# Two transformer blocks on one core: the dense up-projections by Strassen's seven products

## The reference, cut to what matters

```python
D_FF = 2816
def swiglu(h, w1, w3, w2):                                  # layer 0 of the first block
    return (jax.nn.silu(h @ w1) * (h @ w3)) @ w2

def channel_mixer(h, w_up, ffn_dw_w, ffn_dw_b, w_down):     # both layers of the second block
    u = causal_depthwise_conv(h @ w_up, ffn_dw_w, ffn_dw_b) # three taps over the tokens
    a, b = jnp.split(u, 2, axis=-1)
    return (jax.nn.silu(a) * b) @ w_down
```

## Time and profile before

| | |
|---|---|
| median of three runs | 2740.4 us (2736.98 to 2740.84) |
| profiled execution, its own time | 2740.35 us |
| its span, first to last instruction | 2738.2 us |
| granted TensorE clock, mean | 0.994 of full |
| busy share: TensorE, VectorE, ScalarE, GpSimd | 99%, 35%, 19%, 3% |
| the 20 F units of f13 | 296 to 434 us of the span |
| those of up0 | 1983 to 2122 us |
| those of up1 | 2520 to 2659 us |

### The profile page before, as it was taken

The page is one execution under the profiler, slowest core; times in us unless marked ns, Lnnn a source line. Parts: engine busy times, 40 slices in busy tenths (PEclk is TensorE's granted clock), DMA queues, the critical chain, the costliest instruction groups (busy, mean ns, idle before and its releaser), DMA issues. The chain is left out here.

```text
span 2738.2 us, 45257 instructions
## 1 busy us (share of the span) xinstructions
PE 2697.9 (99%) x19261; PEld 2103.6 (77%) x19261; DVE 968.6 (35%) x2203; ACT 528.6 (19%) x1128; POOL 94.2 (3%) x181
## 2 busy tenths in 40 slices
PE   7999999999989999999999999999999999999999
PEld 6788988978978745555546548788988997889888
DVE  2555432366520000001001004676555235744330
ACT  3322100232220001101101103333121024231110
POOL 0000111000100000000000000000011000000000
PEclk9999999999989999999999999999999999999999
DMA  9536675654569998999999995344576643234432
GB/s 371 195 139 246 230 265 215 233 210 162 185 276 427 404 367 352 426 427 409 426 426 408 426 394 226 130 146 174 211 276 237 231 171 139 93 127 158 169 116 100
DMA packets 70328, 706.62 MB, mean 258 GB/s; under 512 B 7793, under 2 KB 8049, under 8 KB 31601
## 3 DMA queue, kind: packets, MB, share of 16 engines
q1 hardware_dynamic: 44640, 610.92, 55.8%
q0 software_dynamic: 25488, 92.81, 9.5%
HBM read 702.65 MB, written 1.05 MB: 257 GB/s over the span
## 5 line engine op out<-in xcount | busy, mean ns | idle before, releaser
L990 PE MATMUL psum<-hT,ring 128*128 128x256 f32 x4544 | 994.4, 380 | 0.0
L990 PEld LDWEIGHTS psum<-hT,ring 128*128 128x128 f32 x4544 | 859.9, 190 | 121.5 <-ACT work L1596 2.0
L990 PE MATMUL psum<-work,ring 128*128 128x256 f32 x1624 | 353.0, 379 | 0.0
L990 PEld LDWEIGHTS psum<-work,ring 128*128 128x128 f32 x1624 | 308.2, 190 | 42.7 <-ACT work L1596 0.7
L2295 DVE CUSTOM_DVE_ANT_0 mod_in<-mod_in,c_rows,cols 128x1024 f32<-128x1024 f32 x152 | 190.8, 1279 | 40.0 <-DMA mod_in<-in_mods 36.7
L1251 PE MATMUL psum<-ring,work 128*32 128x256 f32 x2880 | 186.5, 380 | 0.0
L2256 DVE TENSOR_TENSOR work<-work,psum 128x128 f32<-128x128 f32 x119 | 34.3, 288 | 414.0 <-ACT work L1637 414.0
L2422 POOL DMA_DIRECT2D mod_in<-in_mods x176 | 93.5, 531 | 2464.7 <-DVE ada L2295 2419.2
L1005 PE MATMUL psum<-hT,ring 128*128 128x128 f32 x1408 | 164.7, 279 | 3.0 <-DVE hT L1908 1.9
L1005 PEld LDWEIGHTS psum<-hT,ring 128*128 128x128 f32 x1408 | 162.9, 195 | 3.6 <-DVE hT L1908 2.0
L1261 PE MATMUL psum<-ring,work 128*64 128x256 f32 x1280 | 147.0, 382 | 0.0
(11 more groups left out here) (262 smaller groups left out, 2472.6 us busy)
## 6 DMA issues: line engine op xcount, KB each, us to landing
ring<-in_m SPq DMA_DIRECT2D x112, 2048.0 KB, 16.5
work<-in_m SPq DMA_DIRECT2D x56, 2048.0 KB, 17.6
ring<-in_w_in SPq DMA_DIRECT2D x46, 2048.0 KB, 8.5
mod_in<-in_mods POOLq DMA_DIRECT2D x176, 512.0 KB, 5.4
ring<-in_up SPq DMA_DIRECT2D x22, 2048.0 KB, 8.1
ring<-in_f SPq DMA_DIRECT2D x11, 2048.0 KB, 9.0
ring<-in_down SPq DMA_DIRECT2D x16, 1408.0 KB, 6.7
ring<-in_w_o SPq DMA_DIRECT2D x8, 2048.0 KB, 8.5
```

What stands on the lines that cost most here:

```text
L990: last = mm(gbank(it["bank"])[:, j, :], wt[:, k, col0 + j * P:col0 + (j + 1) * P], rhs[:, k0 + k, :], start=(n == 0), stop=(n == total - 1))
```

## The change

Each of the 60 F units becomes a unit of mode S. Its weights (1024 x 256) and its tokens (1024 x 256) are cut into two by two blocks, and the product of the blocks is formed by seven products of half size instead of eight, in Winograd's form of Strassen's scheme. Each product is four matmuls of 128x128 weights with 128 tokens moving.

- GpSimd makes the sums of weights, four instructions of 128x512 for each unit, one unit ahead of TensorE: three into `MIXED` (room for two units) and one in place in the ring slot.
- VectorE makes the sums of tokens once for each stage, the new item `t_mix`: four instructions of 128x512.
- An S unit takes two of six PSUM banks (`FF_BANKS`). ScalarE copies the first product (128x128), and VectorE adds up the rest with four instructions: 128x256, 128x256, 128x256, 128x128. The silu, the taps and the product of halves come after that. The taps (`fir_rest`) read SBUF instead of PSUM and are put off by one unit.
- Ada items are moved: up0 has 16 instead of 34 and its `down` the next 8; up1 has none instead of 6. The mixer of layer 1 of the second block gets 24.

```diff
+    def s_unit(S, c, col, evac, load, free, first=False, last=False):
+        u = unit([(c, DK, 512, col, 0)], "h", evac, load, free, mode="S")
+        u.update(bank=(ff_bank(), ff_bank()), S=S, mix=state["mixed"], first=first, last=last)
...
-            out.append(unit([(c, DK, 512, 0, 0)], "h", ea, [c], []))
-            out.append(unit([(c, DK, 512, 256, 0)], "h", eb, [], [c]))
+            out.append(s_unit(S, c, 0, ea, [c], [], first=(i == 1)))
+            out.append(s_unit(S, c, 256, eb, [], [c], last=(i == nu - 1)))
...
+            items.insert(2, ph("t_mix", S="a0f", at="a"))
             plan.extend(spread(items, adas(0, 40, 48) + adas(1, 0, 28)))
...
-        if l == 0:
-            rest = adas(2, EARLY_MODS, 48)
+        rest = adas(2 + l, EARLY_MODS, 48)
...
-        plan.extend(spread(items, adas(3, 0, 34) if l == 0 else adas(3, 42, 48)))
+        items.insert(2, ph("t_mix", S=f"b{l}f", at="b"))
+        plan.extend(spread(items, adas(3, 0, 16) if l == 0 else []))
...
+    mixed = [it for it in plan if it["kind"] == "unit" and it["mode"] == "S"]
+    for n, it in enumerate(mixed):
+        it["before"] = mixed[n - 2]["g"] if n >= 2 else None
...
@@ TensorE @@
+            def mixed_unit(it):
...
+                product(one, 0, a[0][0], b11)
+                product(one, 1, a[0][1], b21)
+                if it["first"]:
+                    need(("t_mix", it["S"]))
+                need(("mixed", g, 2))
+                product(one, 2, sum2, t2).then_inc(tensor_done, w.step(("unit_one", g)))
+                if two in ev:
+                    need(ev[two])
+                ev[two] = ("evac", g)
+                product(two, 0, sum1, t1)
+                need(("mixed", g, 3))
+                product(two, 1, a[1][0], t3)
+                need(("mixed", g, 4))
+                product(two, 2, sum4, b22)
+                product(two, 3, a[1][1], t4).then_inc(tensor_done, w.step(("unit", g), *[("used", c["n"]) for c in it["free"]]))
...
@@ ScalarE @@
+            def mixed_unit(it):
...
+                need(("unit_one", g))
+                A(firsts[it["mix"] % 2], hbank(it["bank"][0])[:, 0, :], ACT.Copy).then_inc(scalar_done, w.step(("first", g)))
+                need(("evac", g))
...
@@ VectorE @@
+            def t_mix(it):
...
+                need(("h", S, 0, 3), ("h", S, 1, 3), ("h", S, 1, 7))
+                V.tensor_tensor(t1, b12, b11, ALU.subtract).then_inc(vector_done, w.step())
+                V.tensor_tensor(t3, b22, b12, ALU.subtract).then_inc(vector_done, w.step())
+                dve.wait_ge(vector_done, w.now() - 1)
+                V.tensor_tensor(t2, b22, t1, ALU.subtract).then_inc(vector_done, w.step())
+                dve.wait_ge(vector_done, w.now())
+                V.tensor_tensor(t4, b21, t2, ALU.subtract).then_inc(vector_done, w.step(("t_mix", S)))
...
+            def mixed_unit(it):
...
+                need(("first", g))
+                V.tensor_tensor(out[:, 0:2, :], firsts[it["mix"] % 2].unsqueeze(1).to_broadcast([P, 2, P]),
+                                hbank(one)[:, 1:3, :], ALU.add).then_inc(vector_done, w.step(("evac_one", g)))
+                need(("unit", g))
+                dve.wait_ge(vector_done, w.now())
+                V.tensor_tensor(sums, out[:, 1:2, :].to_broadcast([P, 2, P]), hbank(two)[:, 0:2, :], ALU.add).then_inc(
+                    vector_done, w.step())
+                dve.wait_ge(vector_done, w.now())
+                V.tensor_tensor(out[:, 1:3, :], sums, hbank(two)[:, 2:4, :], ALU.add).then_inc(vector_done, w.step())
+                V.tensor_tensor(out[:, 3, :], sums[:, 1, :], hbank(two)[:, 0, :], ALU.add).then_inc(
+                    vector_done, w.step(("evac", g)))
...
@@ GpSimd @@
+            def mix(it):
...
+                if it["first"]:
+                    pool.wait_ge(vector_done, w.at("x_mul", it["S"], 1, 4))
+                pool.wait_ge(slot_loaded[c["slot"]], w.at("loaded", c["n"]))
+                if it["before"] is not None:
+                    pool.wait_ge(tensor_done, w.at("unit", it["before"]))
+                add(sum1, a21, a22, ALU.add).then_inc(weights_mixed, w.step(("mixed", g, 1)))
+                pool.wait_ge(weights_mixed, w.now())
+                add(sum2, sum1, a11, ALU.subtract).then_inc(weights_mixed, w.step(("mixed", g, 2)))
+                add(a21, a11, a21, ALU.subtract).then_inc(weights_mixed, w.step(("mixed", g, 3)))
+                pool.wait_ge(weights_mixed, w.now() - 1)
+                add(sum4, a12, sum2, ALU.subtract).then_inc(weights_mixed, w.step(("mixed", g, 4)))
...
+                    if it["kind"] == "unit":
+                        while len(made) < len(ahead) and ahead[len(made)]["g"] <= it["g"] + 1:
+                            mix(ahead[len(made)])
+                            made.append(it["g"])
```

More of the change, by code:

```diff
@@ L130 @@
           "rope_tables", "tables", "consts", "mod_cols", "acol", "x_sq", "x_sum", "x_fin", "x_mul", "x_aff", "x_add",
-          "n_add", "c_add")
+          "n_add", "c_add", "t_mix")
+FF_BANKS = (0, 1, 2, 5, 6, 7)
+MIXES = 6
 def make_plan():
-    plan, state = [], {"chunk": 0, "bank": 0, "side": 0, "ada": 0, "fence": 0}
+    plan, state = [], {"chunk": 0, "bank": 0, "side": 0, "ada": 0, "fence": 0, "ff": 0, "mixed": 0}
     def chunk(name, idx, width):
@@ L261, in h_units, with glu_units @@
                      tile=u, ready=ready) for u in range(2)]
-    def glu_units(name, pre, nu, evacs, halves):
+    def glu_units(S, name, pre, nu, evacs, halves):
         out = h_units(chunk(name, pre + (0,), SLOT), DK, "h", halves)
+        for u in out:
+            u["bank"] = ff_bank()
+        out[1]["half_bank"] = out[0]["bank"]
         for i in range(1, nu):
@@ L432, in make_plan @@
             plan.extend(score(z + dq + dk + q + dv + v + hg + gates + pa + pb + o, slots))
-            items = glu_units("f13", (), FF_U, lambda i: (evac("glu_a", i), evac("glu_b", i)),
+            items = glu_units("a0f", "f13", (), FF_U, lambda i: (evac("glu_a", i), evac("glu_b", i)),
                               [evac("glu_h")] * 2)
@@ L548, in make_plan @@
         assert not taps
[L549 to L552 removed]
+        rest = adas(2 + l, EARLY_MODS, 48)
+        for j, it in zip((2, 3, 4, 5) + tuple(22 + 22 * j // (len(rest) - 4) for j in range(len(rest) - 4)), rest):
+            slots[j].append(it)
         slots[28] += [ph("c_add", tag=B, layer=l)]
@@ L970, in unit @@
                 g = it["g"]
[L972 to L975, removed]
+                if it["mode"] == "S":
+                    mixed_unit(it)
+                    return
+                if it["bank"] in ev:
+                    need(ev[it["bank"]])
+                ev[it["bank"]] = ("evac", g)
                 need(*it["ready"])
@@ L1018, in unit, with product @@
                 last.then_inc(tensor_done, w.step(("unit", g), *[("used", c["n"]) for c in it["free"]]))
+            def mixed_unit(it):
+                g, (one, two) = it["g"], it["bank"]
+                c = it["parts"][0][0]
+                a, (sum1, sum2, sum4) = quads(it)
+                b11, b12, b21, b22 = (R["h"][:, 4 * i:4 * i + 4, t * P:(t + 1) * P] for i in range(2) for t in range(2))
+                t1, t2, t3, t4 = TOKENS[it["S"][0]]
+                def product(bank, at, weights, tokens):
+                    for k in range(4):
+                        last = mm(hbank(bank)[:, at, :], weights[:, k, :], tokens[:, k, :], start=(k == 0), stop=(k == 3))
+                    return last
+                if one in ev:
+                    need(ev[one])
+                ev[one] = ("evac_one", g)
+                pe.wait_ge(slot_loaded[c["slot"]], w.at("loaded", c["n"]))
+                product(one, 0, a[0][0], b11)
[13 more added lines that the diff above has]
+                product(two, 3, a[1][1], t4).then_inc(tensor_done, w.step(("unit", g), *[("used", c["n"]) for c in it["free"]]))
             def first_mod(it):
@@ L2345, in run @@
                         acol_of(it)
+                    elif kind == "t_mix":
+                        t_mix(it)
                     elif kind == "x_add":
```

107 lines of the change are left out of this document (102 added, 5 removed).

## The result

The changed kernel takes 2786.0 us (median of four runs, 2783.6 to 2788.2) against 2739.4 us for the kernel before on the same chip: a ratio of 1.0172, with a 95% interval of 1.0159 to 1.0184. It is 1.7% slower. The forecast was 2785 us.

The account below looks back on a forecast made before the run. TensorE was taken to bound the kernel before, and GpSimd, taking turns with VectorE, the changed stages. Terms of 17.7 (f13), 22.9 (up0) and 3.7 us (up1) sum to +44.3 on 2740.35: 2785 us, range 2728 to 2830.

Parts of the forecast that it names:

- the 20 S units: S units of f13, up0 and up1: GpSimd periods of 7.7, 7.9 and 6.9 us, adding 17.7, 22.9 and 3.7 us.
- down-projections: After up0 and up1: the last `hid` tile comes some 5.8 us late, covered by 7.8 us, 2 us to spare; cost nothing.
- the turns that decide it: VectorE instructions with two SBUF inputs and GpSimd's sums exclude each other, lifting GpSimd's period above TensorE's 6.25 us.
- if VectorE's evacuation and not GpSimd is what TensorE waits for: Sign, named beforehand, that the forecast is wrong; it costed VectorE's evacuation, 1.5 us a unit, at nothing.
- TensorE's own work: An S unit takes 6.25 us against an F unit's 6.91, saving 0.66 us a unit, 39.6 us over 60.
- The wait for `t_mix`: First S unit of f13, up0, up1: TensorE waits 4.4, 8.4 and 7.2 us for the token sums.
- GpSimd's sums: Each 128x512 weight sum on GpSimd was taken as 1.22 us, four making 4.9 us a unit.
- The half clock behind them: After each `t_mix` wait TensorE runs at half rate for 4.9 us; first S unit ends 6.9 us after `t_mix`.
- so that GpSimd becomes the bound: In all three stages GpSimd's period with turns, 7.7, 7.9 and 6.9 us, exceeds TensorE's 6.25 us.
- The engines don't meet: Rival: GpSimd stays under 6.25 us a unit in all three stages; sum -12 us, 2728 us; chance 0.16.
- A sum is dearer: Rival: a GpSimd sum takes 1.5 us, with turns, giving periods of 8.9, 9.0 and 7.95 us; 2845 us; chance 0.14.
- They meet half the time: Rival: periods of 6.9, 6.7 and 5.9 us in f13, up0, up1; 2740 us, no change; chance 0.10.

## Why the prediction was right

| | forecast, us | measured, us |
|---|---|---|
| in front of the S units (norm, H units): f13, up0, up1 | 0, 0, 0 | +2.8, +2.8, +4.5 |
| the 20 S units: f13, up0, up1 | +17.7, +22.9, +3.7 | +11.4, +10.0, -0.9 |
| down-projections: f13, up0, up1 | 0, 0, 0 | 0, +7.7, +5.5 |
| mixer with 24 more ada items | 0 | 0.0 |
| elsewhere | 0 | +1.5 |
| sum | +44.3 | +45.2 |

The measured terms are the differences of the starts of the stages' first records, before and after: the S units of up0, for example, start at 1983.54 before and 2002.06 after, 18.5 us later, and their down-projections 28.5 later. For the first row it is the last stretch of H records, 104 of them, which took 11.6 us before and 14.5, 14.5 and 16.1 after. The rounded terms add up to 45.3. The periods between S units and the first unit of each stage with its wait, the only things that were priced, brought 20.5 us and not 44.3. The norm's stalls (10.1 us), which were left out, the down-projections (13.2), which were costed at nothing, and the 1.5 us elsewhere made up for it. So the forecast is right in its sign and in the turns that decide it, but in two of three stages not in the engine that TensorE waits for, and its closeness of 1 us is luck. By a sign that it named itself ("if VectorE's evacuation and not GpSimd is what TensorE waits for") it was wrong in up0 and up1.

**TensorE's own work.** 6.25 us for an S unit were expected, 6.26 came where nothing held it up. Half, six and seven chunks took 19.1, 25.7 and 26.6 us off the kernel before, against 19.8, 23.8 and 27.7 by 0.66 us a unit; the interval of each is wide enough (21.4 to 30.4 us for six).

**The wait for `t_mix`.** Forecast 4.4, 8.4 and 7.2 us; 4.9, 8.2 and 7.0 came (4.2, 8.3 and 7.0 without GpSimd's sums). For f13 the sum of the forecast did not use its 4.4 us but let GpSimd's sums delay `t_mix` by two turns, a wait of 6.8 us; that was 2 us too much. Putting `t_mix` earlier gave 25.6 us back. The half clock behind them was overrated in two of three stages. In up0 the row behind the wait, and the next:

```profile
2012.26 3.41 PE L1074 MATMUL psum<-work 128*128 128x128 f32 x16 [8.25 <-DVE work L1891]
...
2015.50 1.06 PE L1074 MATMUL psum<-work,ring 128*128 128x128 f32 x8
```

The granted clock there was 0.50, the lower of the two levels (columns as in the earlier trace rows):

```profile
2012.20:2015.00 2.80, 2.75 (x13) 2.75 (x14) 0.32 (x1) 0.28 (x1) 0.00 (x0) 0.50 0.00 0
```

The first 16 records took 3.41 instead of 1.95 us and the next eight were already at full rate, so the first unit was through 5.9 us after the wait where the forecast had 6.9 (6.1 in f13, 6.9 in up1). Without the lower clock it would be 4.46; work takes twice as long at it, so it lasted twice what was lost: 2.9 us here, 3.2 in f13, 4.8 in up1, where the forecast had 4.9. This is partly chance: behind the same wait of 8.3 us in up0 the first unit took 7.1 us in the kernel without sums and 7.4 in that without the later taps.

**GpSimd's sums.** 1.22 us was the value taken; a sum alone takes 1.26, and the next one, where it doesn't read that sum, starts 1.22 after it began. The Trainium skill (GPSIMD Engine Reference, section 3.1) led to 1.12 or 1.35; the trace lies between.

**The turns.** The sign hung on them, and they are shown three ways: two instructions of 1.27 us that take 2.25 beside each other, everything back at its length and 57.7 us gone when the sums are left out (one run), and taps untouched where an input is in PSUM. The rule of the Trainium skill (SBUF — State Buffer, "Who interferes with whom") agrees with all three, with 2.25 us against 1.26.

GpSimd paid less for them than the forecast had. Its four sums, 5.0 us when alone, took 6.35 us a unit in f13, 5.8 in up0 and 5.5 in up1 (their rows by form over the three windows above), which is 1.3, 0.8 and 0.5 us more, where every instruction of VectorE's with two SBUF inputs holding GpSimd up would be 2.3, 2.85 and 1.95.

**The step that failed** is "so that GpSimd becomes the bound" in all three stages, and with it the periods of 7.7, 7.9 and 6.9 us. Measured are 7.19, 6.95 and 6.39 us from one unit to the next (f13: (447.94 - 311.34) / 19); from the end of the first unit to that of the last the three stages took 3.8, 12.0 and 4.7 us less than forecast. GpSimd bounds f13 alone: its sums and loads make 7.2 us a unit there. In up0 and up1 they make 6.3 and 5.5, less than the period, and where TensorE waits it waits for banks: VectorE's evacuation, costed at nothing with the remark that its cover is gone "only if turns double it", had its four taps go from 1.79 to 4.40 us. The forecast had counted what a tap costs GpSimd (its own 0.41 us), but not what it pays itself, up to a whole sum of 1.26 us for each short tap. In up0 that is the bound; in up1 the period is only 0.13 us over TensorE's own 6.26. Most of its price was not seen in the period but at the end, where VectorE was two units behind: 5.2 and 3.4 us of waiting in the down-projections, with the clock down again behind both (the lag grew by 7.7 and 5.5 us over them):

```profile
2164.00:2166.00 2.00, 1.86 (x4) 1.51 (x5) 0.08 (x1) 0.00 (x0) 0.00 (x0) 0.50 0.00 0
...
2712.00:2714.00 2.00, 2.00 (x6) 1.55 (x6) 0.00 (x0) 0.00 (x0) 0.00 (x0) 0.50 0.00 0
```

The forecast had 2 us to spare there.

A term was left out: the four tensor_scalar steps of the norm in front of each stage wait for GpSimd's first sums too, 5.2 instead of 1.1 us in up0. TensorE stood 2 us each time (6.1 us over the three stages), and the H unit was 2.8 us later through. In up1, where its clock fell too (0.74 from 2553 to 2556 us, 0.69 to 2559), it was 4.5: the 50 records behind the last such wait took 7.5 us, where the 50 in front of the first took 5.75.

```profile
1991.13 5.18 DVE L2097 TENSOR_SCALAR hT<-hT,acol,ada 128x128 f32<-128x128 f32 x4
...
2553.73 7.48 PE L1050 MATMUL psum<-hT,ring 128*128 128x128 f32 x50 [0.73 <-DVE hT L2097]
```

What makes the 1.5 us elsewhere was not tried. The changed kernel is 0.8 us ahead at f13's H units, and from its down-projection to up0, where the experts' stage lies, 2.3 us are lost; TensorE's waits for loads of `in_m` grew there from 2.1 to 4.2 us. Runs of one kernel differ by more than that.

**The rivals.** "The engines don't meet" gave 2728 us, and the kernel without sums took 2728.3: the working was right and its condition was false. "A sum is dearer" is refuted by 1.26 us. "They meet half the time" had the time wrong (2740), but its periods of 6.9, 6.7 and 5.9 us (6.25 in place of the last, TensorE's own) are nearer to the measured 7.19, 6.95 and 6.39 than the forecast's, and GpSimd did pay only between a quarter and somewhat over half of what full turns would cost. What that rival lacked is what the forecast lacked: VectorE's side of the turns, at the norm and at the end of a stage.

## What to carry to other kernels

Count VectorE's instructions with two inputs in SBUF, and its tensor_scalar between SBUF and SBUF, before giving GpSimd sums, and price both sides: such an instruction can hold a sum up for its own length, and pays up to a whole sum itself, which for a short one is most (0.45 us became 1.10 a tap). Look then at what waits for either engine, at the head and the end of a stage too. Where TensorE is what limits, a saving that costs the side engines more than the unit's time can be taken for a part of the units only: seven of ten chunks gained 26.6 us where all ten lost 46.6, or 18.4 with `t_mix` ahead and the norm spared. And an item's place in an engine's order is a price of its own: `t_mix` one item earlier was worth 25.6 us. Not tried is leaving the taps' input in PSUM, where GpSimd's sums don't touch them.

## What the runs showed of the hardware

A GpSimd sum of 128x512 floats takes 1.26 us, 1.8 times VectorE's 0.69. Beside a VectorE reduction of 1.28 us with two SBUF inputs each lasts nearly as long as both together (2.25 us). A tensor_scalar of 128x128 from SBUF to SBUF, with one tensor input, is held up as well: the four in a row took 5.18 us instead of 1.1, about one for each sum of 1.26. An instruction with one input in PSUM is not: 478 ns with and without. After waits of 4.9, 8.2 and 7.0 us TensorE's records were at the lower clock for 3.2, 2.9 and 4.8 us, worked out as above: the longest wait did not bring the longest stretch. Behind the same wait of 8.3 us in three kernels the stretch was 2.9, 5.3 and 5.9 us, so it can't be told from the wait alone.
